# A one-core decoder step: a rearranged opening (sample scaling on a diagonal, order of the turned halves, sine table, issuer of the state rows)

## What is computed

```python
h = rmsnorm(x, norm1_g)
z = h @ w_in                                   # 1024 x 2824
u_s5, x_rg, g_rg, q, k, v, o, gi, gf = split(z)
y1 = s5_mixer(u_s5, ...)       # step = exp(log_step); a = exp(lam_re*step) * (cos, sin)(lam_im*step); a scan over time
y2 = rglru_mixer(x_rg, g_rg, ...)              # short convolution, gates, a scan
y3 = mlstm_mixer(q, k, v, gi, gf, o, ...)
x = x + concat(y1, y2, y3) @ w_out
x = x + moe(rmsnorm(x, norm2_g), ...)          # top 4 of 32 experts, clamped SwiGLU
return rmsnorm(x, final_norm_g), states
```

## Time and profile before

| | |
|---|---|
| median of 3 runs | 1098.44 us (1097.82 to 1098.92) |
| the profiled execution's own time | 1098.81 us |
| its span, first to last instruction | 1097.0 us |
| PE busy | 1036.5 us (94%) |
| DVE, ACT, POOL busy | 316.1, 197.9, 95.3 us |
| HBM read | 424.68 MB, 390 GB/s over the span |
| chain that ended last | PE 55%, DMA 36%, DVE 5%, ACT 2% |

### The profile page before, as it was taken

The page is one execution under the profiler, slowest core; times in us unless marked ns, Lnnn a source line. Parts: engine busy times, 40 slices in busy tenths (PEclk is TensorE's granted clock), DMA queues, the critical chain, the costliest instruction groups (busy, mean ns, idle before and its releaser), DMA issues.

```text
span 1097.0 us, 13183 instructions
## 1 busy us (share of the span) xinstructions
PE 1036.5 (94%) x5134; PEld 435.2 (40%) x5134; DVE 316.1 (29%) x640; ACT 197.9 (18%) x418; POOL 95.3 (9%) x177
## 2 busy tenths in 40 slices
PE   8999999999999999899889989999899989998997
PEld 5767745334333433343333323333324233433322
DVE  5889456312131212121202112121212121212023
ACT  5543615401110201011000201020102010100002
POOL 6899000000000000000000000000000000000000
PEclk9999999999999999999999999999999999999999
DMA  7533799999999999999999999999999999999995
GB/s 223 194 114 77 260 370 406 427 426 431 430 433 430 430 431 431 431 431 431 434 431 431 431 431 431 431 431 434 431 430 431 431 431 431 431 433 431 424 426 239
DMA packets 62051, 429.45 MB, mean 391 GB/s; under 512 B 12022, under 2 KB 25054, under 8 KB 33342
## 3 DMA queue, kind: packets, MB, share of 16 engines
q1 hardware_dynamic: 60868, 428.16, 93.5%
q10 hardware_dynamic: 1146, 0.79, 0.2%
HBM read 424.68 MB, written 3.67 MB: 390 GB/s over the span
## 4 chain that ended last, share of the span: by engine, by line
PE 55%; DMA 36%; DVE 5%; ACT 2%; issue 1%; SPq 1%; ACTq 0%; DVEq 0%
DMA ring_a<-in_exp_w_dram 27%; PE psum L2405 17%; PE psum L2440 14%; DMA ring_b<-in_exp_w_dram 8%; PE psum L2426 7%; PE psum L2327 3%; PE psum L2158 3%; PE psum L2350 2%; PE psum L1886 2%; PE psum L2449 1%; PE psum L2277 1%; PE psum L2283 1%; DVE rgb L1341 1%; SPq L449 1%; DMA xn<-in_x_prompt_dram 1%
## 5 line engine op out<-in xcount | busy, mean ns | idle before, releaser
L2405 PE MATMUL psum<-ring_a,xg 128*64 128x512 f32 x1200 | 341.8, 600 | 14.4 <-DMA ring_a<-in_exp_w_dram 14.4
L2440 PE MATMUL psum<-ring_a,aT 128*64 128x512 f32 x768 | 217.7, 596 | 8.5 <-DMA ring_a<-in_exp_w_dram 8.2
L2405 PEld LDWEIGHTS psum<-ring_a,xg 128*64 128x64 f32 x1200 | 102.9, 137 | 170.1 <-issue 166.0
L2405 PE MATMUL psum<-ring_b,xg 128*64 128x512 f32 x368 | 152.3, 598 | 7.8 <-DMA ring_a<-in_exp_w_dram 7.8
L1672 DVE TENSOR_TENSOR x<-x,psum 128x512 f32<-128x512 f32 x60 | 41.2, 687 | 367.7 <-PE psum L2350 367.7
L2426 PE MATMUL psum<-ring_a,xg 128*64 128x512 f32 x336 | 103.5, 608 | 14.2 <-DMA ring_b<-in_exp_w_dram 14.2
L2440 PEld LDWEIGHTS psum<-ring_a,aT 128*64 128x64 f32 x768 | 68.0, 137 | 110.2 <-issue 104.3
L2440 PE MATMUL psum<-ring_b,aT 128*64 128x512 f32 x256 | 104.0, 595 | 4.2 <-DMA ring_a<-in_exp_w_dram 2.6
L1760 DVE TENSOR_SCALAR acts<-psum 128x512 f32<-128x512 f32 x32 | 22.0, 688 | 223.3 <-PE psum L2426 207.8
L1045 ACT ACTIVATE acts<-acts 128x512 f32<-128x512 f32 x32 | 20.1, 627 | 296.5 <-DVE acts L1760 296.5
L2405 PEld LDWEIGHTS psum<-ring_b,xg 128*64 128x64 f32 x368 | 43.1, 136 | 75.5 <-issue 63.6
(11 more groups left out here) (508 smaller groups left out, 934.9 us busy)
## 6 DMA issues: line engine op xcount, KB each, us to landing
ring_a<-in_exp_w_dram SPq DMA_DIRECT2D x144, 2048.0 KB, 26.3
ring_b<-in_exp_w_dram SPq DMA_DIRECT2D x46, 2048.0 KB, 24.8
ring_a<-in_w_in_dram SPq DMA_DIRECT2D x4, 2048.0 KB, 8.5
ring_a<-in_w_out_dram SPq DMA_DIRECT2D x2, 2048.0 KB, 9.8
ring_a<-in_w_in_dram SPq DMA_DIRECT2D x3, 1024.0 KB, 5.9
ring_a<-in_state_ml_c_dram SPq DMA_DIRECT2D x4, 512.0 KB, 6.1
out_dram<-ring_a SPq DMA_DIRECT2D x4, 512.0 KB, 6.1
ring_b<-in_exp_w_dram SPq DMA_DIRECT2D x2, 1024.0 KB, 28.5
```

The costliest lines, as they stand in the source:

```text
L2405: m = M(psum[64 * x:64 * x + 64, bk, :], xg[:, k, u, 64 * x:64 * x + 64], w[x][:, 512 * bk:512 * bk + 512], start=False, stop=(k == KD - 1))
L2440: m = M(psum[64 * x:64 * x + 64, 4 + nn, :], aT[:, 2 * j + s, 64 * x:64 * x + 64], w[x][:, 1024 * s + 512 * nn:1024 * s + 512 * nn + 512], ...
```

## The change

For the samples' tile VectorE no longer multiplies the 32x1024 rows. It multiplies the 32x32 corner of the identity by the scale (`scale_diag`, in a corner of `uT_rolled` that is written later), and TensorE multiplies the unscaled rows by this diagonal instead of turning them. The copies of the halves go in the order hT0, hT2, hT4, hT3, hT5 on VectorE, and ScalarE keeps hT1 alone; TensorE starts u0 after the three left halves and waits for the right ones after u0's fourth chunk. Two of the later short matmuls are left out, and one moves. On ScalarE the decay's exponent waits for its own argument and no longer for the reduced angles, and the wait for the angles stands ahead of the sines. The two bias loads move behind the sines, and the five loads of state rows move from SP's queue to ScalarE's, behind them. u1 and the gate products are copied out ahead of the first bias piece, and the state rows last. TensorE turns the state rows inside xr0, after its sixth chunk, instead of between u1 and the gate products. `glw` is issued behind the second block of w_in.

```diff
+        scale_diag = uT_rolled[0:TS, 0, 0:TS]
...
-                    for x, name in enumerate(("state_s5_re", "state_s5_im")):
-                        sp.dma_start(srow[64 * x:64 * x + 64, :], ...).then_inc(sem("par_loaded"), 16)
-                    sp.dma_start(prow[0:32, :], ...)
-                    sp.dma_start(prow[32:48, :], ...)
-                    sp.dma_start(prow[48:96, :], ...)
...
+                if c == 2:
                     sp.dma_start(glw[:], ...)
-                if c == 2:
...
-            for i in range(2):
-                name = f"hT{2 * i + 1}"
-                ...
-            act.dma_start(bias_in[:, 0:512], ...)
-            act.dma_start(bias_in[:, 512:768], ...)
+            await_fill(act, "hT1")
+            for c in range(4):
+                m = A(hT[:, 4 + c, 0:128], bank("hT1")[:, 128 * c:128 * c + 128], ACT.Copy, scale=vec("norm1_g", 4 + c))
+            m.then_inc(drained[FILLS["hT1"][0]], 1)
 
             A(sm[:, 1, :], vecs[:, NVEC:NVEC + J5], ACT.Exp).then_inc(says_now("step_ready"), 1)
-            act.wait_ge(*at("angle_reduced", 1))
+            act.wait_ge(sem("mag_arg"), 1)
             A(sm[:, 5, :], sm[:, 2, :], ACT.Exp).then_inc(says_now("mag_ready"), 1)
...
+            act.wait_ge(*at("angle_reduced", 1))
             A(sm[:, 6, :], sm[:, 9, :], ACT.Sin).then_inc(says_now("angle_ready"), 1)
             A(sm[:, 7, :], sm[:, 8, :], ACT.Sin).then_inc(says_now("angle_ready"), 1)
+            act.dma_start(bias_in[:, 0:512], ...)
+            act.dma_start(bias_in[:, 512:768], ...)
...
             u_out(0)
+            u_out(1)
+            copy_out("gp", gate_parts, bank("gp")[:, 0:T])
             bias_piece(0)
-            u_out(1)
             copy_out("par", parT[:, 0:224], bank("par")[:, 0:224])
-            copy_out("gp", gate_parts, bank("gp")[:, 0:T])
...
-                says(TSC(xn[0:n, i, :], xn[0:n, i, :], nst[0:n, 4 + i:5 + i], None, ALU.mult), "xn_ready", i + 1)
+                if i < 2:
+                    says(TSC(xn[0:n, i, :], xn[0:n, i, :], nst[0:n, 4 + i:5 + i], None, ALU.mult), "xn_ready", i + 1)
+                else:
+                    says(TSC(scale_diag, ident[0:n, 0:n], nst[0:n, 4 + i:5 + i], None, ALU.mult), "xn_ready", i + 1)
...
-            for k in (0, 2, 4, 5):
+            for k in (0, 2, 4, 3, 5):
...
-            dv(TT(sm[:, 2, :], lr, sm[:, 1, :], ALU.mult))
+            TT(sm[:, 2, :], lr, sm[:, 1, :], ALU.mult).then_inc(sem("mag_arg"), 1)
...
+                    if i < 2:
+                        m = TR(bank(f"hT{k}")[:, 128 * c:128 * c + n], rows_, ident[0:n, 0:n])
+                    else:
+                        m = M(bank(f"hT{k}")[:, 128 * c:128 * c + n], rows_, scale_diag, start=True, stop=True)
...
-                if k == 3:
-                    keep_warm(1)
-            keep_warm(2)
-            for k in range(6):
...
+            keep_warm(1)
...
+            rows_turned(0)
             pe.wait_ge(sem("w_in0"), 16)
-            channels("u0", 0, 0)
+            channels("u0", 0, 0, lambda k: rows_turned(1) if k == 3 else None)
             channels("u1", 0, 128)
-            pe.wait_ge(sem("par_loaded"), 16 * 5)
...
             pe.wait_ge(sem("wgate_loaded"), 16)
             gate_products()
             pe.wait_ge(sem("w_in0_right"), 16)
-            channels("xr0", 0, 256)
+            channels("xr0", 0, 256, state_rows)
```

## The result

The changed kernel takes 1106.38 us (median of 4, 1105.17 to 1107.74) beside 1098.62 (4) for the kernel before on the same chip: 1.0065 of it, interval 1.0046 to 1.0083. The forecast was 1097.3, range 1095.8 to 1098.9: it was wrong, and on the slow side, for which only rival (d) stood, with 0.10.

A forecast was written before the change was run, and what follows sets the result against it. The bound was the transfer stream's start, set by TensorE's o2; gains of 0.95 on TensorE and 1.65 left on VectorE were limited at the sigmoids to 1.1 us, from 1098.44 to 1097.3 us, range 1095.8 to 1098.9.

The forecast's parts named there:

- rival (d): ScalarE's queue is blocked by its seven issues, a loss from 6.5 us together on; 1103 to 1108 us; chance 0.10.
- The anchor: The end stands at the start of the unbroken transfer stream, opened by the second w_out issue, plus bytes over rate.
- The opening: Up to the sines: u0 at 12.5 instead of 13.46 on TensorE, sines done at 15.87 instead of 18.21.
- the rows at 27.36 and 29.77: ScalarE's table load at 27.36, its gates' exponent at 29.77: evidence that a wait written ahead doesn't hold the load back.
- rival (b): ScalarE's table load still waits for the angles, sines end at 17.15, VectorE gains 1.07; 1097.4 us; chance 0.05.
- I take no stall: these go on another queue: State loads on ScalarE's queue reach TensorE's turning inside xr0 in time; 6.2 us landing would stall it 1 us.
- I take nothing: its rows are few and long: The bias load's landing costs VectorE nothing at the bias piece; 7.5 us landing would leave it a gain of 0.6.
- From there both carry 1.1: From TensorE's wait for VectorE's scan, near 75.4 us, both engines run 1.1 us early through to o2.
- TensorE's wait of 1.21 ends 1.1 early: At 75.4 us TensorE arrives 0.95 early and its wait for VectorE's scan to free banks ends 1.1 early.
- The forecast's sum: o2 and the second w_out issue 1.1 us earlier, at 127.2; profiled execution 1097.7, median 1097.3 us; chance 0.58.

The follow-up runs named there:

- r3: The changed kernel with the state loads back on SP ahead of w_in and the bias loads ahead of ScalarE's first exponent; median 1105.59 us.
- r5: The kernel before with only the sines' part: the magnitudes' exponential waits for its own argument, the angles' wait stands ahead of the sines; median 1104.36 us.
- r1: The changed kernel, but SP issues the second w_in block and all behind it only after the five state loads have landed; median 1103.69 us.
- r7: r3 with fourteen one-column memsets (2.4 us in all) ahead of GpSimd's table; median 1098.64 us.
- r15: The whole changed kernel with the second w_in block held until the state rows land and ten memsets (1.7 us) holding GpSimd; median 1100.13 us.
- r18: r15 with five more idle matmuls on TensorE in the opening; median 1098.95 us.
- r2: The changed kernel, but the gate's and glu weights wait on SP for the state loads while the second w_in block goes early; median 1104.71 us.
- r12: The kernel before with only the moves of the loads, and the state rows turned inside xr0; median 1108.38 us.
- r16: The kernel before with six small reductions (1.89 us) on VectorE ahead of its fifth scan; median 1103.92 us.

## Why the prediction was wrong, point by point

- **The anchor was right.** The end is the second w_out issue plus 970 to 972 us in 19 of 20 profiles.
- **The opening was right, with small misses.** The diagonal's operation took 0.44 us instead of 0.17 and the sixteen passes 1.97 instead of 0.7; u0 still came at 12.29 (12.5). The table load was moved as argued from the rows at 27.36 and 29.77, which settles rival (b); no drain stood behind it, so the 2.66 us of the Trainium skill ("ScalarE: Activation LUTs", What ACT_TABLE_LOAD costs) do not show here: load from 13.79 to 15.07, sine at 15.45 on VectorE's word. The seven issues ended at 20.95 (19.4), one of 2.00 among them.
- **The step that failed first: "I take no stall: these go on another queue".** I noted that the next w_in block goes out nearly 3 us earlier and counted it as free. It moved 5.1 us (21.07 to 15.96), past the state rows, and the loads were in flight beside it. The bound that I had (6.2 us for small loads behind a block) was the right kind of row, and even that was short: 6.5 to 9.5. The same step failed for the bias loads, at "I take nothing: its rows are few and long". Issued from 15.46, they let ScalarE go at 28.20, some 12 us later, where 7.5 was the most that I allowed for. By the profile of after this holds VectorE 3.2 us, more than the state rows then add (1.1). What the Trainium skill says of packet-wise turns ("DMA: Bandwidth & Descriptors", Queues, rings and completion order) tipped me; four of the five loads did land ahead of the block (25.0 to 28.6 against 30.2), as turns would have it, but turns did not make them early. Rival (d) did not happen as written: the seven issues took 5.5 us together, under the 6.5 from which it reckoned a loss. Only its last sentence named the road, a state load that lands after 8 us, and I gave it no room in the range.
- **The step that failed behind it: "From there both carry 1.1".** I shifted every operation by the gain of its chain and left its duration. On VectorE and GpSimd the duration depended on what the other was doing: 1.04 us instead of 0.17 for a step of 14 columns, 1.80 instead of 0.56 for a product of scores. So 2.35 us for GpSimd and 1.65 for VectorE was no gain (r3, r5): GpSimd kept its part, VectorE paid it back. In after this made 4.32 us into 12.49, and the second w_out came at 136.63 instead of the 127.2 forecast.
- **"TensorE's wait of 1.21 ends 1.1 early"** was that step's consequence. In r3 it was 3.73 and cost the clock. I treated a short wait as slack to be used up, not as one that a head start on one side and a delay on the other both lengthen.
- **The forecast's sum was reached** in the profiled executions of r1 and r7: w_out at 127.21 and 127.14, 1097.67 and 1097.82. For r1 that is luck, the fastest of ten; r7, all ten of which lie within 1.8 us, has the state loads back on SP and GpSimd held back, so it is another kernel. Its median is 0.1% under before, which can't be told from no change.

## What to carry to other kernels

When a small load is taken from a queue, price what moves up in its place: the transfer behind it starts earlier and may land on the load itself. Where two engines hold each other up, as VectorE and GpSimd do here, moving one changes the durations of both: look which of their operations overlap after the move, above all those that both start at the same event. Before speeding up a producer, look at how long it will then wait, and whether its clock survives that wait.

## What the runs showed of the hardware

- Loads of 24 to 32 KB took 1.8 to 2.5 us on SP's queue ahead of the block, 3.1 to 4.4 behind two bias loads on ScalarE's queue with the block held back (r1, r15, r18), 6.3 to 11.1 beside a 2 MB block on another queue (after, r2, r12).
- VectorE's product with two SBUF inputs: 0.56 us free, 1.80 when GpSimd's 1.41 us multiplication had started 0.03 us before. Once the two waited for the same scan, the delay came again in every block to the end of the loop (1.77 to 1.79 us in all four products of r16).
- Waits of 2.05 to 4.43 us for the first scans left TensorE at a lowered clock (0.50 to 0.94) in eight profiles, waits of up to 1.72 did not; a wait of 3.10 us from 95 us on in r16 did not either.
